# Attention values as the stationary operand, two heads per pair of matmuls, and row sums moved into the gate

## The reference

```python
h = rmsnorm(x, norm_even[i])
(qa, ka, va, ga, ...) = _split(h @ w_in_even[i], EVEN_SPLIT)
# per block of 128 queries and per head (8 heads of 64):
logits = q.k * scale + bias, -inf where the indexer did not choose the key
p = jax.nn.softmax(logits, axis=-1)
o_a = einsum('bhqk,bqkhd->bqhd', p, vs)
o_a = o_a * jax.nn.silu(ga)
...                                   # o_b: gated linear attention, normed and gated
x = x + jnp.concatenate([o_a, o_b], axis=-1) @ w_out_even[i]
```

## Time and profile before

| | |
|---|---|
| median of 3 runs | 532.03 us (531.91 to 532.03) |
| profiled execution, its own time | 531.84 us |
| its span, first to last instruction | 530.1 us |
| TensorE busy (weight loads) | 517.0 us, 98% (414.5 us, 78%) |
| VectorE busy | 372.9 us, 70% |
| ScalarE busy | 238.9 us, 45% |
| GpSimd busy | 291.9 us, 55% |

### The profile page before, as it was taken

The page is one execution under the profiler, slowest core; times in us unless marked ns, Lnnn a source line. Parts: engine busy times, 40 slices in busy tenths (PEclk is TensorE's granted clock), DMA queues, the critical chain, the costliest instruction groups (busy, mean ns, idle before and its releaser), DMA issues.

```text
span 530.1 us, 7516 instructions
## 1 busy us (share of the span) xinstructions
PE 517.0 (98%) x2807; PEld 414.5 (78%) x2807; DVE 372.9 (70%) x770; ACT 238.9 (45%) x374; POOL 291.9 (55%) x180
## 2 busy tenths in 40 slices
PE   7999999999999899999999999999999999999994
PEld 7876888777777788888888889778777677787883
DVE  3795699588876356656461054999989999869824
ACT  6734743333311144644451445456555554267413
POOL 5460765755533066656414316599999998351701
PEclk9999999999999999999999999999999999999998
DMA  8443463312222002200263403602322222402004
GB/s 264 136 130 117 124 220 94 106 60 75 80 80 80 1 0 81 81 0 1 83 237 105 132 1 102 176 2 80 85 82 79 77 77 80 156 1 80 1 0 159
DMA packets 42386, 46.75 MB, mean 88 GB/s; under 512 B 3176, under 2 KB 30851, under 8 KB 42350
## 3 DMA queue, kind: packets, MB, share of 16 engines
q1 hardware_dynamic: 42350, 46.28, 27.7%
HBM read 44.03 MB, written 2.12 MB: 87 GB/s over the span
## 4 chain that ended last, share of the span: by engine, by line
PE 84%; DVE 10%; ACT 2%; issue 2%; POOL 1%; POOLq 0%; ACTq 0%; DVEq 0%
PE bank L1509 30%; PE bank L1529 29%; PE bank L1812 3%; PE bank L1654 3%; PE bank L1722 3%; DVE r_va L1070 2%; PE bank L1699 2%; DVE top L1068 2%; PE bank L1800 2%; PE bank L1711 2%; DVE r_ob L1054 1%; PE bank L1818 1%; PE bank L1545 1%; PE bank L1593 1%; PE bank L1444 1%
## 5 line engine op out<-in xcount | busy, mean ns | idle before, releaser
L535 POOL TENSOR_TENSOR w_lo<-w_raw,w_hi 128x2048 fp32r<-128x2048 f32 (+1 forms) x31 | 140.3, 4528 | 103.1 <-ACT w_hi L682 102.2
L1509 PE MATMUL bank<-hT_hi,w_hi 128*128 128x512 f32 (+1 forms) x280 | 112.5, 402 | 0.0
L1509 PE MATMUL bank<-hT_hi,w_lo 128*128 128x512 f32 (+1 forms) x280 | 111.0, 396 | 0.0
L1509 PE MATMUL bank<-hT_lo,w_hi 128*128 128x512 f32 (+1 forms) x280 | 111.0, 396 | 0.0
L1529 PE MATMUL bank<-w_hi,hT_hi 128*128 128x512 f32 x252 | 102.6, 407 | 0.1
L1529 PE MATMUL bank<-w_hi,hT_lo 128*128 128x512 f32 x252 | 98.5, 391 | 0.0
L1529 PE MATMUL bank<-w_lo,hT_hi 128*128 128x512 f32 x252 | 98.3, 390 | 0.0
L682 ACT ACTIVATE w_hi<-w_raw 128x2048 fp32r<-128x2048 f32 (+1 forms) x35 | 65.7, 1879 | 41.7 <-PE bank L1529 37.0
L1326 DVE SCALAR_TENSOR_TENSOR bank<-r_va,pvec,bank 128x512 f32<-128x512 f32 x108 | 76.0, 748 | 0.9
L615 POOL TENSOR_TENSOR r_g<-r_g 128x512 f32<-128x512 f32 x48 | 62.0, 1291 | 11.4 <-ACT r_g L868 5.6
L1509 PEld LDWEIGHTS bank<-hT_lo,w_hi 128*128 128x128 f32 (+1 forms) x280 | 52.3, 187 | 14.2 <-issue 3.4
(11 more groups left out here) (232 smaller groups left out, 791.5 us busy)
## 6 DMA issues: line engine op xcount, KB each, us to landing
w_raw<-in_w_in_even_dram SPq DMA_DIRECT2D x14, 1024.0 KB, 5.3
w_raw<-in_w_in_odd_dram SPq DMA_DIRECT2D x16, 512.0 KB, 4.7
w_raw<-in_w_out_even_dram SPq DMA_DIRECT2D x4, 1024.0 KB, 8.3
w_raw<-in_w_in_odd_dram SPq DMA_DIRECT2D x4, 1024.0 KB, 5.1
w_raw<-in_w_out_odd_dram SPq DMA_DIRECT2D x4, 1024.0 KB, 5.1
r_x<-in_x_dram SPq DMA_DIRECT2D x4, 512.0 KB, 6.0
r_x<-bias_rows SPq DMA_DIRECT2D x4, 512.0 KB, 5.9
r_x<-in_x_dram SPq DMA_DIRECT2D x1, 2048.0 KB, 8.0
```

The costliest lines, as they stand in the source:

```text
L535: nc.gpsimd.tensor_tensor(v(w_lo[j % 3]), v(w_raw[j % 2]), v(w_hi[j % 3]).bitcast(F32), ALU.subtract).then_inc(lo_ready, 1)
L1509: ins = nc.tensor.matmul(proj_bank(g)[0:m, :], w[:, k, P * i:P * i + m], h[:, k, :], start=(n == 0), stop=(n == 3 * KC - 1))
```

## The change

- pv becomes pv_two_heads(p) for heads 2p and 2p+1: the values of a head (128 keys x 64) are the stationary operand, the transposed probabilities (128x128) stream, and the output is 64 partitions x 128 columns: head 2c in partitions 0 to 63 of bank 7, head 2c+1 in 64 to 127. It runs in attend(n) for even n only.
- probT has four buffers (two of them in r_att).
- empty_oa is a plain copy into oaT, which holds the attention output transposed. The row sums divide the gate instead: gates_by_sums multiplies gate_a by the reciprocals, three row blocks at once, then the fourth.
- At the end TensorE transposes the blocks of ob first, then runs the last pair, then transposes the blocks of gate_a (not of oa); VectorE multiplies each of the four banks in place by oaT (gated_transposed), and ScalarE and VectorE split the product into hT_hi and hT_lo. VectorE writes the low parts of chunks 4 to 7 before it empties bank 7 for the last time. The fourth gate transpose, the first into bank 7, waits for that (oa_emptied).

```diff
--- before.py
+++ after.py
@@ -228,7 +228,9 @@
         TABLE_HEADS = {6: (0, 2), 7: (2, 4), 8: (4, 6), 9: (6, 8)}
         logit = [r_g[:, 512 * i:512 * i + 512] for i in (0, 1)]
         prob = [r_g[:, 1024 + 512 * i:1536 + 512 * i] for i in (0, 1)]
-        probT = [r_g[:, 2048 + 512 * i:2560 + 512 * i] for i in (0, 1)]
+        probT = [r_g[:, 2048 + 512 * i:2560 + 512 * i] for i in (0, 1)] + \
+            [r_att[:, 512 * i:512 * i + 512] for i in (0, 1)]
+        oaT = r_oa[:].rearrange("p (c t) -> p c t", c=4)
         masked = [r_g[:, 3072 + 512 * i:3584 + 512 * i] for i in (0, 1)]
         sq_b = [r_att[:, 512 * i:512 * i + 512] for i in range(TB)]
         conv_y = lambda c: (r_oa if c < 4 else r_ob)[:, 512 * (c % 4):512 * (c % 4) + 512]
@@ -338,6 +340,7 @@
         probT_ready = sem("probT_ready")
         pv_done = sem("pv_done")
         oa_emptied = sem("oa_emptied")
+        gated_T = sem("gated_T")
         gates_silu = sem("gates_silu")
         u_ready = sem("u_ready")
         conv_done = sem("conv_done")
@@ -681,11 +684,14 @@
                     v = lambda t: t[:]
                 nc.scalar.activation(v(w_hi[j % 3]), v(w_raw[j % 2]), ACT.Copy).then_inc(hi_ready, 1)
 
-            def hT_high(base, order, bank_of, scale):
-                for n, c in enumerate(order):
-                    act.wait_ge(hT_in_bank, base + n + 1)
-                    nc.scalar.activation(hT_hi[:, c, :], bank[bank_of(n)][:], ACT.Copy,
-                                         scale=scale(c)).then_inc(hT_hi_ready, 1)
+            def mixed_high(n, c):
+
+                if c < 4:
+                    act.wait_ge(gated_T, c + 1)
+                else:
+                    act.wait_ge(hT_in_bank, R_MIX + n + 1)
+                nc.scalar.activation(hT_hi[:, c, :], bank[mixed_bank(n)][:], ACT.Copy,
+                                     scale=1.0 if c < 4 else pb3[:, 2:3]).then_inc(hT_hi_ready, 1)
 
             def half_high(base, half, half_bank, scale, chunks=range(KC)):
 
@@ -826,7 +832,8 @@
             empty(FIRST[S_GA] + TB - 1, gate_a[:, TB - 1, :], func=ACT.Silu)
 
             wait_slot_used(act, S_OE - 1)
-            hT_high(R_MIX, B_FIRST, mixed_bank, lambda c: 1.0 if c < 4 else pb3[:, 2:3])
+            for n, c in enumerate(B_FIRST):
+                mixed_high(n, c)
 
 
             def row_squares(base, n0, half, squared=lambda t: None, rows=range(TB)):
@@ -967,12 +974,18 @@
                     nc.vector.scalar_tensor_tensor(out=v, in0=half_sq[:, TB + t:TB + t + 1], scalar=1.0 / D,
                                                    in1=v, op0=ALU.mult, op1=ALU.add).then_inc(var_ready, 1)
 
-            def hT_low(base, order, bank_of, scale):
-                for n, c in enumerate(order):
-                    dve.wait_ge(hT_hi_ready, base + n + 1)
-                    nc.vector.scalar_tensor_tensor(
-                        out=hT_lo[:, c, :], in0=bank[bank_of(n)][:], scalar=scale(c),
-                        in1=hT_hi[:, c, :].bitcast(F32), op0=ALU.mult, op1=ALU.subtract).then_inc(hT_ready, 1)
+            def mixed_low(n, c):
+                dve.wait_ge(hT_hi_ready, R_MIX + n + 1)
+                nc.vector.scalar_tensor_tensor(
+                    out=hT_lo[:, c, :], in0=bank[mixed_bank(n)][:], scalar=1.0 if c < 4 else pb3[:, 2:3],
+                    in1=hT_hi[:, c, :].bitcast(F32), op0=ALU.mult, op1=ALU.subtract).then_inc(hT_ready, 1)
+
+            def gated_transposed(n, c):
+
+                dve.wait_ge(hT_in_bank, R_MIX + n + 1)
+                dve.wait_ge(oa_emptied, TB)
+                b = bank[mixed_bank(n)][:]
+                nc.vector.tensor_tensor(b, b, oaT[:, c, :], ALU.mult).then_inc(gated_T, 1)
 
             def half_low(base, half, half_bank, scale, chunks=range(KC)):
                 for c in chunks:
@@ -1188,12 +1201,18 @@
 
             def empty_oa(tb):
 
-                dve.wait_ge(pv_done, AH * (tb + 1))
-                link(nc.vector.reciprocal(row_inv[:, AH * tb:AH * tb + AH], row_sum[:, AH * tb:AH * tb + AH]))
-                inv = row_inv[:, AH * tb:AH * tb + AH].unsqueeze(2).to_broadcast([P, AH, AD])
-                nc.vector.tensor_tensor(oa[:, tb, :].rearrange("p (h d) -> p h d", h=AH),
-                                        bank[7][:].rearrange("p (h d) -> p h d", h=AH), inv,
-                                        ALU.mult).then_inc(oa_emptied, 1)
+                dve.wait_ge(pv_done, AH // 2 * (tb + 1))
+                nc.vector.tensor_copy(oaT[:, :, P * tb:P * tb + P],
+                                      bank[7][:].rearrange("p (c q) -> p c q", c=4)).then_inc(oa_emptied, 1)
+
+            def gates_by_sums(t0, t1):
+
+                h0, h1 = AH * t0, AH * t1
+                dve.wait_ge(prob_ready, h1)
+                link(nc.vector.reciprocal(row_inv[:, h0:h1], row_sum[:, h0:h1]))
+                rows = gate_a[:, t0:t1, :].rearrange("p t (h d) -> p (t h) d", h=AH)
+                inv = row_inv[:, h0:h1].unsqueeze(2).to_broadcast([P, h1 - h0, AD])
+                nc.vector.tensor_tensor(rows, rows, inv, ALU.mult).then_inc(mixed_a, 1)
 
             logits(0)
             logits(1)
@@ -1202,9 +1221,9 @@
                     logits(n + 2)
                 w = P * (n // AH + 1)
                 dve.wait_ge(probT_done, n + 1)
-                if n >= 2:
-                    dve.wait_ge(pv_done, n - 1)
-                nc.vector.tensor_copy(probT[n % 2][:, 0:w], bank[6][:, 0:w]).then_inc(probT_ready, 1)
+                if n >= 4:
+                    dve.wait_ge(pv_done, n // 2 - 1)
+                nc.vector.tensor_copy(probT[n % 4][:, 0:w], bank[6][:, 0:w]).then_inc(probT_ready, 1)
                 if n % AH == 0 and n:
                     empty_oa(n // AH - 1)
                 if n < TB:
@@ -1229,15 +1248,17 @@
                         [P, BH, DV]), ALU.mult))
 
             dve.wait_ge(gates_silu, 2)
-            dve.wait_ge(oa_emptied, TB - 1)
-            nc.vector.tensor_tensor(oa[:, 0:TB - 1, :], oa[:, 0:TB - 1, :], gate_a[:, 0:TB - 1, :],
-                                    ALU.mult).then_inc(mixed_a, 1)
+            gates_by_sums(0, TB - 1)
+            dve.wait_ge(act_emptied, evacs_through(FIRST[S_GA] + TB - 1, "act"))
+            gates_by_sums(TB - 1, TB)
+            for n in range(4):
+                mixed_low(n, B_FIRST[n])
             empty_oa(TB - 1)
-            dve.wait_ge(oa_emptied, TB)
-            dve.wait_ge(act_emptied, evacs_through(FIRST[S_GA] + TB - 1, "act"))
-            nc.vector.tensor_tensor(oa[:, TB - 1, :], oa[:, TB - 1, :], gate_a[:, TB - 1, :],
-                                    ALU.mult).then_inc(mixed_a, 1)
-            hT_low(R_MIX, B_FIRST, mixed_bank, lambda c: 1.0 if c < 4 else pb3[:, 2:3])
+            for n in range(4, KC):
+                gated_transposed(n, B_FIRST[n])
+                if n > 4:
+                    mixed_low(n - 1, B_FIRST[n - 1])
+            mixed_low(KC - 1, B_FIRST[KC - 1])
 
 
             def residual(s0, variance, scaled_rows, added=lambda t, half: None):
@@ -1427,17 +1448,6 @@
         @block.tensor
         def _(pe):
             pe.wait_ge(pool_chain, 2)
-            def transpose_blocks(order, blocks, ready, bank_of):
-
-                for n, t in blocks:
-                    ready(n, t)
-                    ins = nc.tensor.transpose(bank[bank_of(n)][:, P * t:P * t + P], hx(t, order[n]), ident[:])
-                    if t == TB - 1:
-                        ins.then_inc(hT_in_bank, 1)
-
-            LOW, HIGH = range(4), range(4, KC)
-            ROWS_1 = [(n, t) for part in (LOW, HIGH) for t in range(TB) for n in part]
-
             def keep_clock(n, dst):
 
                 for _ in range(n):
@@ -1711,22 +1721,27 @@
                     ins = nc.tensor.transpose(bank[6][:, P * i:P * i + P], prob[n % 2][:, P * i:P * i + P], ident[:])
                 ins.then_inc(probT_done, 1)
 
-            def pv(n):
-                tb, h = divmod(n, AH)
-                pe.wait_ge(probT_ready, n + 1)
-                if n == 0:
+            def pv_two_heads(p):
+
+                tb, c = divmod(p, AH // 2)
+                pe.wait_ge(probT_ready, 2 * p + 2)
+                if p == 0:
                     pe.wait_ge(act_emptied, evacs_through(FIRST[S_VA] + 3, "act"))
-                if h == 0 and tb:
+                if c == 0 and tb:
                     pe.wait_ge(oa_emptied, tb)
                 for i in range(tb + 1):
-                    ins = nc.tensor.matmul(bank[7][:, AD * h:AD * h + AD], probT[n % 2][:, P * i:P * i + P],
-                                           va[:, i, AD * h:AD * h + AD], start=(i == 0), stop=(i == tb))
+                    for r in range(2):
+                        h = 2 * c + r
+                        ins = nc.tensor.matmul(bank[7][AD * r:AD * r + AD, P * c:P * c + P],
+                                               va[:, i, AD * h:AD * h + AD],
+                                               probT[(2 * p + r) % 4][:, P * i:P * i + P],
```

(33 more changed lines are left out.)

## The result

| | before | after |
|---|---|---|
| median | 532.02 us (8 runs) | 535.05 us (8 runs) |
| ratio, 95% interval | | 1.006 (1.0042 to 1.0077) |
| profiled execution, its own time | 531.84 us | 536.76 us |
| its span | 530.1 us | 535.0 us |

The change makes the kernel 3.0 us slower, 0.6%. The profiled execution of after lies 1.7 us above the median, because its clock fell a second time, around 478 us in the layer norm of layer 1.

A forecast was written before the change was run, and what follows sets the result against it. TensorE's instruction order was taken to bound the kernel (busy 98%). An end loss of 2.65 us minus a loop gain of 2.6 gave +0.05, 531.9 us against the profiled execution, 532.1 us as median; range 531.0 to 534.8.

The forecast's parts named there:

- a balance of gain and stall: Main case, whole kernel: the loop's gain of 2.6 us against the end's loss of 2.65, +0.05 us; chance 0.66.
- the low clock: Rival, TensorE's stall at the end of attention: clock falls to 0.50, costing 1.5 to 2.0 us, 533.9 us; chance 0.25.
- loop, up to the transposes of step 29: Attention loop, 14 pairs: 13.8 us removed, 0.7 left behind, 10.5 added, a gain of 2.6 us (1.2 to 3.3).
- order at the end, without the clock: End of attention: TensorE stands 3.9 us for bank 7's copy; slot 16 starts 2.65 us later (2.2 to 3.2).
- the cover that was given to them: After attention: chunks 0 to 3 have 5 us before slot 17; GpSimd ends about 285, slot 18 starts 295.8; no wait.
- a sign of being wrong: Prediction wrong if bank 7's wait is under 3 or over 5 us, the clock falls, or transposes meeting qk_pair cost over 0.13.
- what hides the rest of the loop: Attention loop: probT copies, the wait for probT_ready and emptying bank 7 have cover and cost nothing.
- the joints: Around the pair's block: 0.08 us at its entry, some 0.02 at its exit, 0.05 where transposes meet qk_pair in odd steps.
- The price of the half calls: New value matmuls in the loop: a block of k half calls costs 0.25 + 0.055 k us, 1.13 us for 16.
- The lower bound of 1.2 us: Smallest loop gain: 0.13 us for the meeting and 0.074 us a half call without a fixed part.
- the meeting: Odd steps, transposes directly ahead of qk_pair: 0.05 us of the old 0.13 stays, bounds 0 and 0.13.
- no overlap: Rival, loop's value matmuls: the two halves do not overlap, half calls cost 0.112 us, +7.3 in all, 539.4 us; chance 0.04.

The follow-up runs named there:

- the kernel with 60 matmuls: The changed kernel with 60 small bf16 matmuls on TensorE in front of the unchanged wait for bank 7: 533.56 us, ratio to before 1.0022.
- The traces without the wait for the exp: Changed kernel emptying bank 7 first, exps of steps 18 and 19 ahead of slot 16's split (529.59 us); same exp edit alone on the kernel before (531.93 us).
- The heads apart: The version emptying bank 7 first, with all key blocks of one head, then all of the other, instead of in turns: 533.34 us, ratio to before 1.0022.
- moving one line: The changed kernel with VectorE emptying bank 7 right behind the first gate product, ahead of the second and the low parts: 530.71 us, ratio to before 0.997.

## Why the prediction was wrong

It said 532.1 us, a balance of gain and stall, and gave the low clock a chance of 0.25 with 533.9 us. Two terms failed, by about the same amount: the clock behind the stall, put at nothing in the sum, cost 1.5 us, and the loop gained 1.05 us and not 2.6. The sum by its own terms:

| term | forecast | measured |
|---|---|---|
| loop, up to the transposes of step 29 | -2.6 (-3.3 to -1.2) | -1.05 |
| order at the end, without the clock | +2.65 (2.2 to 3.2) | +2.5 |
| clock behind the stall | 0, or +1.5 to 2.0 at a chance of 0.25 | +1.5 |
| sum | +0.05 | +2.95 (of +3.03) |

*The order at the end was right.* The wait of the fourth gate transpose, its cause, and VectorE's queue came out as worked out: 3.5 us where 3.9 stood, and 12.45 us instead of 9.96 from step 29 to slot 16 in the kernel with 60 matmuls (260.36 to 272.81). Slots 17 and 18 had the cover that was given to them: no wait of TensorE is listed there.

*The clock* was one failure, and one that the prediction had named as a sign of being wrong. The rival's mechanism and price were right (1.5 us in place of 1.8), and 535.05 lies in the range that it gave for it, but its chance was too small. It did not decide the sign alone: with the stall filled the kernel is still slower, 1.0022 (1.0007 to 1.0038). I had a row for it: 3.05 us from the last matmul work to the fall, less than the stall I forecast. I argued it down with the 32 old transposes at 1.00, but they are work, and a stall is none; the run with transposes in the stall shows that they hold the clock as matmuls do. The Trainium skill (TensorE: Matmul & The Clock Gate, Part 4) says that transposes do not count as busy in the same way; the fp32 transposes here do, by the row above of 268 to 276 us at 1.00. The same page, Why this matters for your kernels, warns of idle gaps between bursts of matmuls; the traces agree, with the clock at 0.50 behind the waits of 2.2 and 3.5 us.

*The loop's gain was put too high, for two reasons,* 1.05 us in place of 2.6, which is outside the bounds too. First, the step "what hides the rest of the loop" looked at VectorE and at the semaphores of the pairs, and not at ScalarE, whose exp of step 18 was only just in time: it held the old loop by 0.17 us and the new one by 0.78, so 0.61 us of the gain went into that wait. Second, the joints. The price of the half calls was right (1.02 us for a block of 16; 1.13 forecast, of which 0.10 for its joints). But the transposes need 0.53 us up to the pair's block and up to qk_pair (257.45 to 257.98; 254.36 to 254.89), where the old ones needed 0.43 up to the values: 0.10 us at each of two joints in every pair, while the sum had 0.08 and 0.05. That is 0.07 x 14 = 1.0 us. The traces without the wait for the exp bear this out: the loop gains 78.43 - 76.77 = 1.66 us there, 0.94 less than forecast. No run changed the joints alone. The lower bound of 1.2 us doesn't follow from the terms that it names either: 0.074 us a half call without a fixed part is cheaper than 0.25 + 0.055 k, and with 0.13 us for the meeting it gives 2.5 us; 0.13 with the main price gives 1.4.

*The range* reached to 534.8 and missed 535.05: it covered the fall with the loop at its forecast gain, or the weak loop without the fall (533.56 us measured), not the two together (its loop bound of -1.2 with the fall would have given 533.9 + 1.4 = 535.3).

The rival "no overlap" (539.4) was wrong, as the starts 0.055 us apart show. The heads apart lose part of that and come to 533.34 us.

## What to carry to other kernels

An instruction that empties a buffer for the engine that bounds the kernel goes ahead of everything on its queue that has slack; moving one line here is 4.3 us, more than the 1.7 us that the new matmul form gives in the loop. When a step becomes faster, look at the other engines' queues at each step of the loop for the one that was only just in time, not at their mean load. And a stall of the bound engine is priced with the low clock behind it: where a stall can't be avoided, matmuls or fp32 transposes in it buy the clock back, as both did here.

## What the runs showed of the hardware

- TensorE's clock was at 0.50 behind waits of 2.2 us and of 3.5 us. After 2.2 us 10 of 12 executions had a low mean clock, six of them with two falls, and after 3.5 us 8 of 8; the kernel without the wait has 26 of 82. With 1.6 us 8 of 12 had one, and no trace shows where. One fall costs 1.5 us here.
- The clock also falls where TensorE is busy: to 0.50 for a stretch between 475 and 481 us, in the layer norm of layer 1, in three profiles. What brings it about there was not tried.
- fp32 transposes hold the clock: 1.00 through 48 of them in a row.
- Two fp32 matmuls with 64-column weights on the two column halves follow each other at 0.055 us a half call if they alternate key block by key block, and at 0.087 us head by head; the old form, with 64 moving columns, took 0.112 us.
- Four fp32 transposes take 0.53 us up to a block in column or row halves, 0.43 us up to the old whole-array values and 0.35 us up to a 512-column matmul (260.50 to 260.85).
